# Feed-forward up projection: weights move in rows of 512 columns, the sums come back to channels by quadrant copies and a block transpose

## The reference

```python
def rmsnorm(x, w):
    return x * lax.rsqrt(jnp.mean(x * x, axis=-1, keepdims=True) + EPS) * w

def conv_glu_ffn(hn, w_up, conv_w, conv_b, w_down):
    up = causal_dwconv(hn @ w_up, conv_w, conv_b)      # 3 taps, per channel
    gate, val = jnp.split(up, 2, axis=-1)
    return (jax.nn.silu(gate) * val) @ w_down
...
    h = h + merged @ w_out[i]
    hn = rmsnorm(h, norm_ffn_w[i])
    h = h + conv_glu_ffn(hn, w_up[i], conv_ffn_w[i], conv_ffn_b[i], w_down[i])
return rmsnorm(h, norm_final_w)
```

## Time and profile before

| | |
|---|---|
| median of 3 runs | 1710.41 us |
| the profiled execution | 1710.42 us, of it 1708.8 us from its first to its last instruction |
| TensorE (PE) busy | 1696.9 us |
| VectorE (DVE) busy | 1335.8 us |
| ScalarE (ACT) busy | 936.8 us |
| the up stage, from the last matmul of out (960.7) to the first of down (1452.1) | 491 us |
| granted clock of TensorE over the span | 0.998 |

### The profile page before, as it was taken

How to read it: one execution, slowest core, us unless ns; L and a number is a source line. 1 busy time by engine, 2 the same in 40 slices (tenths; PEclk the granted TensorE clock), 3 DMA queues, 4 the chain that set the end, 5 groups by cost and what they waited for, 6 DMA issues and landing times.

```text
span 1708.8 us, 27860 instructions
## 1 busy us (share of the span) xinstructions
PE 1696.9 (99%) x9566; PEld 1450.6 (85%) x9566; DVE 1335.8 (78%) x1825; ACT 936.8 (55%) x1182; POOL 159.4 (9%) x262
## 2 busy tenths in 40 slices
PE   9999999999999999999999999999999999999997
PEld 8888888888888888888888888888888888888886
DVE  8999999999999996545666788888888888544544
ACT  7766676666566666444545644544444544434432
POOL 7834101110000000000001000000000000000000
PEclk9999999999999999999999999999999999999999
DMA  7654555545566656555565555555555555555553
GB/s 253 214 175 164 193 180 181 175 165 186 171 209 232 204 192 207 196 190 193 185 234 185 174 195 196 185 186 184 186 193 196 186 184 183 197 193 188 187 191 116
DMA packets 112003, 324.87 MB, mean 190 GB/s; under 512 B 13712, under 2 KB 14912, under 8 KB 111808
## 3 DMA queue, kind: packets, MB, share of 16 engines
q1 hardware_dynamic: 106880, 310.99, 54.6%
q0 software_dynamic: 4336, 12.07, 2.1%
q10 hardware_dynamic: 720, 0.93, 0.2%
HBM read 321.77 MB, written 2.17 MB: 190 GB/s over the span
## 4 chain that ended last, share of the span: by engine, by line
PE 71%; DVE 3%; ACT 0%; issue 0%; DVEq 0%; ACTq 0%
PE psum L1493 32%; PE psum L1495 16%; PE psum L1515 7%; PE psum L1517 7%; PE psum L1516 7%; DVE wlo L931 1%; PE psum L1614 1%; DVE dec L1222 1%; DVE bc L1112 0%; PE psum L1615 0%; DVE vn L1464 0%; PE psum L1639 0%; PE psum L1534 0%; PE psum L1683 0%; PE psum L1528 0%
## 5 line engine op out<-in xcount | busy, mean ns | idle before, releaser
L931 DVE TENSOR_TENSOR wlo<-raw,whi 128x1024 fp32r<-128x1024 f32 x580 | 710.8, 1232 | 325.9 <-ACT whi L541 325.6
L541 ACT ACTIVATE whi<-raw 128x1024 fp32r<-128x1024 f32 x580 | 611.7, 1058 | 440.6 <-PE psum L1495 298.9
L1493 PE MATMUL psum<-nw,whi 128*128 128x512 f32 x1536 | 483.2, 396 | 0.8 <-DVE wlo L963 0.8
L1493 PE MATMUL psum<-act,whi 128*128 128x512 f32 x1280 | 403.4, 396 | 0.3 <-DVE wlo L931 0.2
L1495 PEld LDWEIGHTS psum<-nw,wlo 128*128 128x128 f32 x1536 | 288.5, 188 | 68.2
L1495 PE MATMUL psum<-nw,wlo 128*128 128x256 f32 x1536 | 301.8, 278 | 0.0
L1495 PEld LDWEIGHTS psum<-act,wlo 128*128 128x128 f32 x1280 | 240.5, 188 | 56.8
L1495 PE MATMUL psum<-act,wlo 128*128 128x256 f32 x1280 | 251.5, 278 | 0.0
L1493 PEld LDWEIGHTS psum<-nw,whi 128*128 128x128 f32 x1536 | 233.9, 189 | 1.6 <-issue 1.0
L1493 PE MATMUL psum<-ff,whi 128*128 128x512 f32 x688 | 216.1, 395 | 0.0
L1493 PEld LDWEIGHTS psum<-act,whi 128*128 128x128 f32 x1280 | 194.8, 189 | 4.2 <-issue 2.4
(11 more groups left out here) (229 smaller groups left out, 1769.3 us busy)
## 6 DMA issues: line engine op xcount, KB each, us to landing
raw<-in_w_up SPq DMA_DIRECT2D x176, 512.0 KB, 4.3
raw<-in_w_zx SPq DMA_DIRECT2D x96, 512.0 KB, 3.5
raw<-in_w_down SPq DMA_DIRECT2D x88, 512.0 KB, 4.1
raw<-in_w_gate SPq DMA_DIRECT2D x64, 512.0 KB, 4.9
raw<-in_w_proj SPq DMA_DIRECT2D x48, 512.0 KB, 4.3
raw<-in_w_bc SPq DMA_DIRECT2D x32, 512.0 KB, 3.5
raw<-in_w_glu SPq DMA_DIRECT2D x32, 512.0 KB, 3.6
raw<-in_w_out SPq DMA_DIRECT2D x32, 512.0 KB, 4.0
```

Of the source, the lines that this page charges most:

```text
L541: fn(whi[:, s, :], raw[:, s, :], ACTF.Copy).then_inc(hi_ready, 1)
L931: V.tensor_tensor(wlo[:, s, :], raw[:, s, :], whi[:, s, :], ALU.subtract).then_inc(lo_ready, 1)
L1493: mm(psum[:, b + t, :], whi[:, s, cols(t)], x, start=first, stop=False)
```

## The change

The up stage becomes token-major. A chunk is 8 units and two groups, and there are 22 (`N_UP`). In a unit TensorE runs 12 matmuls of 512 columns in place of 8 of 512 and 8 of 256, and all three products add up in one bank. The loads (the same number and size) bring each partition two runs of 512 values in place of one of 1024.

The sums of a chunk now lie as 128 tokens by 512 columns in two banks. ScalarE copies them into `quad` in 16 pieces, each from one quadrant of 32 partitions to another (`quadrants`), spread over slots 0 to 4 of the next chunk (3, 3, 3, 4, 3). One `V.transpose` of 128 x 1024 on VectorE, in 32 x 32 blocks, then gives four channel tiles in `cpad4` (slot 5), followed by one multiply by the root for all four. `take_hsum` and `add_halves` are gone from this stage. The convolution of a chunk's first group comes in slot 6 and its SiLU, product and parts in slots 6 and 7. Those of the second group follow in slots 0 to 3 of the chunk after. What belongs to the last chunk is moved into the first group of the down stage (`up_end`, slots 0 to 8). TensorE waits for `up_free` of the chunk before the last. POOL clears `cpad4` once, and its second clearing of `sqacc` waits for the last transpose.

```diff
--- before.py
+++ after.py
 PHASES = {"u0": (1, 4, 1), "u": (3, 4, 3), "zx": (24, 4, 4), "bc": (8, 4, 4), "gate": (16, 4, 2),
           "proj": (8, 6, 2), "glu": (16, 2, 2), "out": (8, 4, 2), "up": (44, 4, 2), "down": (8, 11, 4)}
-TOKEN_MAJOR = ("gate", "proj", "glu")
+TOKEN_MAJOR = ("gate", "proj", "glu", "up")
...
+        quad = at("quad", [P, 4, 2, 4, 32], F32, 185 * K)
+        cpad4 = at("cpad4", [P, 4, L + 4], F32, 191 * K)
...
+        up_free, up_turned, cpad4_ready = map(sem, ("up_free", "up_turned", "cpad4_ready"))
...
+                if name == "up":
+                    w = a["w_up"].rearrange("(c g q) p (h n) -> c q h p g n", g=2, q=quads, h=2)
+                    with sp.Fori(0, groups // 4) as i:
+                        for j in range(4 * quads):
+                            n, c, q, half = UNIT0[name] + j, j // (2 * quads), j % (2 * quads) // 2, j % 2
+                            sp.wait_ge(lo_ready, i * (4 * quads) + (n - RING + 1))
+                            sp.dma_start(raw[:, n % RING, :].rearrange("p (g n) -> p g n", g=2),
+                                         w[ds(i * 2 + c, 1), q, half].rearrange("o p g n -> (o p) g n")
+                                         ).then_inc(w_in[n % RING], 16)
+                    continue
...
+            nc.gpsimd.memset(cpad4[:, :, :], 0.0).then_inc(cpad4_ready, 1)
...
                 if n == 0:
                     pool.wait_ge(glu_free, 8)
                 else:
-                    pool.wait_ge(sum_ready, GROUP0["down"])
+                    pool.wait_ge(up_turned, N_UP)
                 nc.gpsimd.memset(sqacc[:, :, :], 0.0).then_inc(sqacc_ready, 1)
...
+                    if name == "down" and i == 0 and r == 0:
+                        up_end(j)
...
+            QUADRANTS = [(q, j) for q in range(4) for j in range(4)]
+            def quadrants(c, cc, first, last):
+                if first == 0:
+                    act.wait_ge(unit_used, c * 8 + (UNIT0["up"] + 8))
+                    if not (isinstance(c, int) and c == 0):
+                        act.wait_ge(up_turned, c)
+                sums_at = chunk_banks("up", cc).rearrange("p t (s j b) -> p t s j b", s=4, j=4)
+                for q, j in QUADRANTS[first:last]:
+                    ins = fn(quad[32 * j:32 * j + 32, :, :, q, :].rearrange("p s t b -> p t s b"),
+                             sums_at[32 * q:32 * q + 32, :, :, j, :], ACTF.Copy)
+                    if (q, j) == QUADRANTS[-1]:
+                        ins.then_inc(up_free, 1)
...
+            def ff_silu(g, to):
                 act.wait_ge(conv2_done, g + 1)
-                fn(tsum[:, 0, :], tsum[:, 0, :], ACTF.Silu).then_inc(silu2_done, 1)
...
+            def ff_hi(g, frm, skip):
                 act.wait_ge(f_sum, g + 1)
-                fn(ff[:, ds(g + skip, 1), 0:L], tsum[:, 0:1, :], ACTF.Copy).then_inc(f_hi, 1)
...
-            def up_turn(i, r, prev, skip=0):
-                _, per, quads, u0, g0 = phase("up")
-                for j in range(4):
-                    split_hi(u0 + r * 4 + j + RING, i * 8)
-                    if prev is not None and j == 0:
-                        ff_silu(prev)
-                    if prev is not None and j == 2:
-                        ff_hi(prev, skip)
-                    if prev is None and j == 2:
+                fn(ff[:, ds(g + skip, 1), 0:L], frm[:, 0:1, :], ACTF.Copy).then_inc(f_hi, 1)
+            def up_step(j, c, cc, second=None, first=None, skips=(0, 0)):
+                parts = (0, 3, 6, 9, 13, 16)
+                if c is not None and j < 5:
+                    quadrants(c, cc, parts[j], parts[j + 1])
+                if second is not None and j == 1:
+                    ff_silu(second, hsum)
+                if second is not None and j == 2:
+                    ff_hi(second, hsum, skips[0])
+                if first is not None and j == 6:
+                    ff_silu(first, tsum)
+                if first is not None and j == 7:
+                    ff_hi(first, tsum, skips[1])
+            def up_turn(i, cc, *steps):
+                u0 = UNIT0["up"] + cc * 8
+                for j in range(8):
+                    split_hi(u0 + j + RING, i * 16)
+                    up_step(j, *steps)
+                    if steps[0] is None and j == 5:
                         act.wait_ge(ns_ready, 2)
                         root(D_MODEL, rs_ready, GROUPS + 2)
-                take_hsum(g0 + r, u0 + (r + 1) * 4, i * 2, i * 8)
...
+            up_turn(0, 0, None, 1)
+            up_turn(0, 1, 0, 0, None, 0)
+            def up_pair(i, skips):
+                up_turn(i, 0, i * 2 - 1, 1, i * 4 - 3, i * 4 - 2, skips[:2])
+                up_turn(i, 1, i * 2, 0, i * 4 - 1, i * 4, skips[2:])
+            with act.Fori(1, 4) as i:
+                up_pair(i, (0, 0, 0, 0))
+            up_pair(4, (0, 0, 0, KT))
+            with act.Fori(5, N_UP // 2) as i:
+                up_pair(i, (KT, KT, KT, KT))
...
+            def up_end(j):
+                up_step(j, N_UP - 1, 1, 2 * N_UP - 3, 2 * N_UP - 2, (KT, KT))
+                if j == 8:
+                    ff_silu(2 * N_UP - 1, hsum)
+                    ff_hi(2 * N_UP - 1, hsum, KT)
...
-            def ff_product(g):
+            def ff_product(g, to):
...
+                V.tensor_tensor(to[:, 0, :], to[:, 0, :], to[:, 1, :], ALU.mult).then_inc(f_sum, 1)
+            def ff_lo(g, frm, skip):
                 dve.wait_ge(f_hi, g + 1)
                 to = ff[:, ds(g + skip, 1), :]
-                V.tensor_tensor(to[:, :, L:2 * L], tsum[:, 0:1, :], to[:, :, 0:L], ALU.subtract).then_inc(f_lo, 1)
+                V.tensor_tensor(to[:, :, L:2 * L], frm[:, 0:1, :], to[:, :, 0:L], ALU.subtract).then_inc(f_lo, 1)
...
-            def up_turn(i, r, prev, skip=0):
-                _, per, quads, u0, g0 = phase("up")
-                for j in range(4):
-                    split_lo(u0 + r * 4 + j + RING, i * 8)
-                    if prev is not None and j == 1:
-                        ff_product(prev)
-                    if prev is not None and j == 3:
-                        ff_lo(prev, skip)
-                add_halves(cpad[:, :, 3:3 + L], g0 + r, i * 2)
-                dve.wait_ge(sum_ready, i * 2 + (g0 + r + 1))
+            def up_turned_back(c):
+                dve.wait_ge(up_free, c + 1)
+                V.transpose(cpad4[:, :, 3:3 + L], quad[:, :, :, :, :].rearrange("p s t q b -> p s (t q b)")
+                            ).then_inc(up_turned, 1)
+                dve.wait_ge(up_turned, c + 1)
                 dve.wait_ge(rs_ready, 2)
-                mul(cpad[:, :, 3:3 + L], cpad[:, :, 3:3 + L], wide_rs(2))
-                conv_pair([tsum[:, t, :] for t in range(2)], i * 4 + 2 * r, 3, "conv_f_w", "conv_f_b", conv2_done)
+                mul(cpad4[:, :, 3:3 + L], cpad4[:, :, 3:3 + L], wide_rs(4))
+            def ff_conv(g, to, half):
+                conv_pair([to[:, t, :] for t in range(2)], g * 2, 3, "conv_f_w", "conv_f_b", conv2_done,
+                          frm=cpad4[:, 2 * half:2 * half + 2, :])
+            def up_step(j, c, second=None, first=None, skips=(0, 0)):
...
+                if second is not None and j == 0:
+                    ff_conv(second, hsum, 1)
+                if second is not None and j == 2:
+                    ff_product(second, hsum)
+                if second is not None and j == 3:
+                    ff_lo(second, hsum, skips[0])
+                if c is not None and j == 5:
+                    up_turned_back(c)
+                if c is not None and j == 6:
+                    ff_conv(2 * c, tsum, 0)
+                if first is not None and j == 7:
+                    ff_product(first, tsum)
+                    ff_lo(first, tsum, skips[1])
+            def up_turn(i, cc, *steps):
+                u0 = UNIT0["up"] + cc * 8
+                for j in range(8):
+                    split_lo(u0 + j + RING, i * 16)
+                    up_step(j, *steps)
+            dve.wait_ge(cpad4_ready, 1)
...
+            up_turn(0, 1, 0, None, 0)
+            def up_pair(i, skips):
+                up_turn(i, 0, i * 2 - 1, i * 4 - 3, i * 4 - 2, skips[:2])
+                up_turn(i, 1, i * 2, i * 4 - 1, i * 4, skips[2:])
...
+            def up_end(j):
+                up_step(j, N_UP - 1, 2 * N_UP - 3, 2 * N_UP - 2, (KT, KT))
+                if j == 7:
+                    ff_conv(2 * N_UP - 1, hsum, 1)
+                if j == 8:
+                    ff_product(2 * N_UP - 1, hsum)
+                    ff_lo(2 * N_UP - 1, hsum, KT)
...
-            def unit_tokens(name, c, j, act):
+            def unit_tokens(name, c, j, act, i=0):
                 n = UNIT0[name] + c * (2 * PHASES[name][1]) + j
-                pe.wait_ge(lo_ready, n + 1)
-                if j == 0:
+                pe.wait_ge(lo_ready, i * 16 + (n + 1))
+                if j == 0 and name == "up":
+                    if isinstance(i, int):
+                        pe.wait_ge(sum_ready, GROUP0["down"] - 1 + c)
```

(32 more changed lines are left out.)

51 lines of the change are left out of this document (8 added, 43 removed).

## The result

The changed kernel takes 1765.48 us, the kernel before 1710.58 in the same set of runs: a ratio of 1.0319, with a 95% interval of 1.0307 to 1.0331. That is 54.9 us more. The profiled execution took 1765.37.

The account below looks back on a forecast made before the run. The helpers' round trip (23.66 us a chunk) was taken to replace TensorE as the bound: 22.7 + 1.4 + 9.3 + 1.5 = +34.9 us on 1710.42, 1745 us; own range 1725 to 1760 (chance 0.60), stated range 1712 to 1770.

Parts of the forecast that it names:

- the helpers' round trip: Up stage: ScalarE and VectorE hand-overs from one transpose to the next take 23.66 us a chunk, over TensorE's 21.84.
- the slow transpose: Rival: transpose takes 2.44 us, round 24.88, up stage +47.6 us, 1772 us in all; chance 0.14.
- TensorE: 2.73 us a unit: Up stage: 176 units at 0.057 us less would save 10.1 us if TensorE stayed the bound.
- ScalarE's unbroken piece: Slots 2 to 5 of up: two splits at 0.96 and seven copies at 0.286 run without a wait, 3.92 us.
- Transpose 1.22, multiply 1.22: VectorE's part of the up round: both priced like a subtraction of that size, 2.60 us with gaps.
- The other nine copies: Copies outside ScalarE's piece without waits: they stand where ScalarE would wait for VectorE anyway, and cost nothing.
- The lead of 5.7 us: Start of up: the ring's lead lasts three rounds at 1.82 us lost each, so four chunks take 21.84 us.
- Up +22.7 us: Up stage: four chunks at 21.84 us and 18 at 23.66, 513.3 us against 490.6.
- Start of down: First group of down: last round +1.4 us, TensorE's wait for ff before unit 10 +9.3, lower clock +1.5.
- TensorE stays the bound: Rival: round at most 21.84 us, saving of 10.1 arrives, wait of 5.9 us in down, 1706 us; chance 0.12.
- Cheap moves: Rival: copies at 0.175 us and transpose 0.69 make the round 22.35, still the bound; 1714 us; chance 0.12.
- Copies cost more than their nearest row: Rival: 0.386 us a copy without overlap adds 0.7 a round, 1759 us; inside the forecast's own range, no separate chance.

Follow-up runs that it names:

- the spread order: Changed kernel with SiLUs, products and ff parts of both groups a slot or more later, one copy moved from slot 2 to 1: 1707.71 us, ratio 0.9981.
- overlapping copies: Changed kernel with the seven copies of slots 3 and 4 as contiguous 128x256 ones to spare places from the second chunk on: 1748.32 us, 1.0219.
- the doubled transpose: Changed kernel with a second transpose per chunk into a spare place that nothing reads: 1790.75 us, 1.0468.

## Why the prediction was right, and where it was short

I forecast 1745 us, slower, by the helpers' round trip and a wait at the start of down. Both are there. The measured 1765.48 lies inside the stated 1712 to 1770, but 5 us above the 1725 to 1760 that I gave this mechanism: the stated range holds it only because it was widened for the slow transpose, which did not occur. That part is luck.

- *TensorE: 2.73 us a unit, -10.1 us if it stayed the bound.* Right, as the spread order shows, which is free of waits: 479.6 us for 176 units, 2.725 each, 11.7 less than the 491.3 of before. The Trainium skill, "TensorE: Matmul & The Clock Gate", section "Back-to-back issue gap", gives 2.59 for the unit of 12 matmuls; the trace differs again.
- *The round trip: 23.66 us.* The mechanism was right, the term of ScalarE's unbroken piece was mis-sized. I put its two splits and seven copies at 3.92 us and they take 4.78, since quadrant copies don't overlap. That is 0.86 of the 0.89 us that the round was longer. With overlapping copies the round was 23.72. The bound of 0.386 us without overlap stood in the prediction (1759 us), but I left out that a split and the copy behind it lose the overlap as well. A row could have warned me: the two copies of the earlier trace rows also go from one half of the partitions to the other, and I read only their durations. In the timeline of the kernel before, the two take 0.57 us together, twice 0.275 and a gap: they don't overlap.

```profile
26.58 0.57 ACT L597 ACTIVATE tsum<-psum 64x128 f32<-64x128 f32 x2
```

- *Transpose 1.22, multiply 1.22, 2.60 with their gaps.* Right: 1.24 and 1.22, and 1.28 and 1.35 from start to start (1222.19, 1223.47, 1224.82), 2.63 together.
- *The other nine copies cost nothing.* Right, within the 1 us between 1765.48 and 1766.43.
- *The lead of 5.7 us hides the first rounds.* The size was right: at 2.71 us lost a round, 22 rounds would be 59.6 us, and the stage lost 531.6 - 480.5 (22 times 21.84) = 51.1, so 8.5 us were hidden: the first chunk, 2.7, and 5.7 us of lead. But I wrote that transposes would be 21.8 apart before the fifth, and they are 24.3 from the first. The helpers spend the lead from the start; only TensorE's waits come later.
- *Up +22.7 us.* It was +40.3. With overlapping copies it was 515.8 - 491.3 = +24.5, so 15.8 of the 17.6 us missing are the mis-sized term.
- *Start of down: +1.4, a wait of 9.3 and 1.5 for the clock, 12.2 in all.* It was +14.6. The wait was 9.57 us, at 1532.19, ended by ff_lo as named. The clock was under-sized: it took 2.4 us (below) where I had 1.5. I had 1.4 for the last round. By the starts, unit 10 begins 40.1 us behind the first matmul of down (1492.1 to 1532.19), where ten units at 2.79 take 27.9: 12.2 us late, which with the clock's 2.4 is the 14.6. The view of the waits has 9.57 and 1.7 of the 12.2; the rest is short waits that modelled ends cover. Windows of the changed kernel around it (length, busy us of PE, PEld, DVE, ACT, POOL, granted clock):

```profile
1530.00:1532.00 2.00, 0.00 (x0) 0.00 (x0) 1.52 (x3) 0.95 (x3) 0.00 (x0) 0.50 0.00 0
1532.00:1533.00 1.00, 0.81 (x2) 0.72 (x3) 0.41 (x2) 0.62 (x1) 0.00 (x0) 0.50 0.78 176
...
1536.00:1537.00 1.00, 1.00 (x4) 0.85 (x4) 0.00 (x0) 0.00 (x0) 0.00 (x0) 0.50 0.75 307
1537.00:1538.00 1.00, 1.00 (x8) 0.86 (x7) 0.00 (x0) 0.45 (x1) 0.00 (x0) 0.98 0.01 4
```

  At 0.50, the lower level of 1.2 GHz, TensorE worked from 1532.19 to about 1537.0, and half the rate for 4.8 us costs 2.4. In the spread order, behind a wait of 6.33 us, down was 253.8 - 244.9 = 8.9 us longer, so the clock cost 2.6.
- *The rivals.* "TensorE stays the bound" was put at 1706 us with a wait of 5.9 us. That didn't happen here, but it is what the spread order does: 1707.7 us and 6.33. "Slow transpose" gave 1772, near the result, by a cause that was not there (1.24 us each). "Cheap moves" asked for copies at 0.175 us, where they are 0.385 apart. "Copies cost more than their nearest row" named the cause that did occur, at 1759 us, and short by the lost overlap of the splits.

## What to carry to other kernels

Where two engines work in order and hand to each other several times a round, add up the distances along one round from start to start, and compare that with the bound's own time; sums of busy time didn't tell 1699 from 1765 us, with the same work in both. When the round is too long, look for the order first: leave a slot between a producer and its consumer, so that neither waits for something just begun. And price the gaps as carefully as the instructions: a few overlaps of 0.10 us that did not come about cost 17 us over 22 rounds.

## What the runs showed of the hardware

- On ScalarE, back-to-back copies overlapped by 0.10 us only while source and target stayed in the quadrants of the last read and write: 0.27 us apart for 32 x 256 on the same partitions, 0.38 where either changes. The splits around such copies lose it too (1.07 in place of 0.96 from a split to the copy behind).
- A 128 x 1024 fp32 block transpose on VectorE takes 1.24 us, as long as a subtraction of that size (1.22 in the mean), and not twice as long.
- Behind waits of 9.57 and 6.33 us TensorE ran at the lower clock for about the same time, 4.8 and 4.7 us, and lost 2.4 to 2.6 us by it. The waits of up to 1.5 us in the up stage of the changed kernel were not followed by a lower clock (1.00 over the stage). With the doubled transpose, where they reach 2.0 us, the clock did fall in the stage. The window below stands behind a wait of 1.85 us at 1166.94. The rounds are no longer for it: the one with this window takes 25.58 us, and the mean is 25.68.

```profile
1170.00:1171.00 1.00, 1.00 (x3) 0.75 (x3) 1.00 (x4) 0.98 (x2) 0.00 (x0) 0.50 0.11 43
```
